# The last expert's down products in an encoder layer with a routed MoE, taken one group of tokens at a time

## The chip, the cores and the metric

One core of one Trainium2 chip. The metric is the device time of one execution in microseconds, the median of several runs.

## What is computed

One encoder layer for two sets of tokens with shared weights, 256 prompt tokens and 512 sample tokens of width 2048: a mixer (latent attention beside a gated DeltaNet), then an expert-choice MoE. Only the MoE's end matters here:

```python
aff = softmax(xt @ w_router)                    # 16 experts
gates, idx = top_k(aff.T, C)                    # C = 2*T/16: 32 prompt and 64 sample tokens for each expert
xe = xt[idx]
h = silu(xe @ w_gate) * (xe @ w_up)             # 2048 -> 1024
ye = (h @ w_down) * gates                       # 1024 -> 2048
out = zeros.at[idx].add(ye)                     # and the residual on top
```

Everything is float32. The 96 tokens of an expert (64 of the sample, 32 of the prompt) are one batch in the kernel, in three groups of 32: groups 0 and 1 are sample tokens, group 2 is the prompt's.

## The kernel before, in words

The program runs five stages one after the other on all engines; the last is `moe` (L2620). It takes the 16 experts in turn.

**Weights.** SP streams them into a ring of six slots (`ring`, RING = 6), 2 MB a unit. The slots lie in two buffers of earlier stages, so the trace names them `wbuf` and `x`. An expert has 12 units: eight of gate and up weights (`load_up`, L2677) and four of down weights (`load_down`, L2686). One unit is two DMAs of 1 MB that count on one semaphore per slot. Before it fills a slot again SP waits (`room`, L2673) until TensorE has used what was there (`s_u`, one count for each unit used) and until the slot's earlier loads have landed. A unit of down weights holds 256 of the 1024 rows of w_down, two steps of 128 rows.

**Order.** The units come in the order: up units of expert e+1, then down units of expert e, in a loop over 15 experts (L2695), and last the four down units of expert 15 (L2698). TensorE follows the same order (L2747 to L2754): up(e+1), down(e), and at the end up(15), down(14), down(15). Its loop body holds two experts, seven rounds of it, so it branches back six times.

**The products.** TensorE is split into four column tiles of 32: a matmul has 32 tokens as its stationary operand and 512 columns of weights as the moving one, and four of them (`j`, J = 4) fill the 128 partitions of one PSUM bank with the four quarters of the 2048 output columns. In the trace each float32 matmul has two records. `down` (L2721) waits for `s_th`, the transposed hidden values `hT`. Then it goes unit by unit: for each unit wait until it has landed (L2725), for each of its two steps and each group g the four matmuls into bank 3 + g (L2733). Each bank sums over eight steps f = 0 to 7. Before a group's first step it waits until DVE has emptied the bank (`s_ye`, L2731).

**After the products.** DVE's `output` (L2796) copies the expert's gates into a column, waits until `ye` is free (`s_free`) and until TensorE has used the fourth down unit (`s_u`, L2801), and scales the three banks into `ye`, one instruction a group (L2803), with a count of `s_ye` after each. POOL's `scatter` (L2836) waits for each group's count on its own and issues one indirect DMA that adds 128 rows of 512 values (32 tokens in four quarters) to `y_sample` or `y_prompt` (L2841). After the third it waits until all three have landed (L2843) and frees `ye`. There is one `ye`, so the scatters of expert 14 must have landed before expert 15's values are scaled.

The first three units of expert 0 were multiplied in part in the stage before; their group 2 is done by the helper `expert_unit` (L719, matmul at L726), whose matmuls into one bank follow one another.

Of the kernel before, what the change touches and what calls it, by code (L numbers as in the profile page):

```python
# [36 lines left out]
NE, FF = 16, 1024  # L37
# [80 lines left out]
class Kernel:  # L118
# [18 lines left out]
    def sb(self, name, shape, dt=F32, ctx=None):  # L137
        return (ctx or self.ctx).enter_context(self.nc.sbuf_tensor(name, shape, dt))

    def sem(self, name, ctx=None):  # L140
        return (ctx or self.ctx).enter_context(self.nc.semaphore(name))


def bcast(ap, axis, n):

    shape = list(ap.unsqueeze(axis).shape)
    shape[axis] = n
    return ap.unsqueeze(axis).to_broadcast(shape)
# [570 lines left out]
def expert_unit(k, u, groups):  # L719

    m = k.ring[u].rearrange("p (x k c j r) -> p x k c j r", x=2, k=2, j=4, r=32)
    for kk in range(2):
        q = 2 * u + kk
        for g in groups:
            for j in range(4):
                last = k.nc.tensor.matmul(k.psum[32 * j:32 * j + 32, g, :].rearrange("p (x c r) -> p x c r", x=2, r=32),  # L726
                                          k.xeT[:, 0, q, 32 * g:32 * g + 32], m[:, :, kk, :, j, :],
                                          start=(q == 0), stop=(q == KD - 1))
    return last
# [1890 lines left out]
def moe(k):  # L2620


    nc, a, ps = k.nc, k.a, k.psum
    UNITS, RING = 12, 6


    G, J = CT // 32, 4

    with ExitStack() as c:
        sb = lambda n, s, dt=F32: k.sb(n, s, dt, c)  # L2630
        sem = lambda n: k.sem(n, c)
        ring = k.ring
        xeT = k.xeT
        h = sb("h", [P, G, FF // J])
        hT = sb("hT", [P, G, FF // P, 32])
# [7 lines left out]
        s_w = k.s_ring  # L2643
        s_u = sem("unit_used")
# [4 lines left out]
        s_th = sem("hidden_transposed")  # L2649
# [3 lines left out]
        s_ye = sem("expert_output")  # L2653
# [12 lines left out]
        loaded = lambda e, w: k.ring_base[w % RING] + e * 64 + 32 * (w // RING + 1)  # L2666

        used = lambda e, w: e * UNITS + w + 1

        with nc.Block() as block:  # L2670
# [29 lines left out]
            @block.tensor  # L2700
            def _(pe):
                def up(ex, e, w0, half, u0=0):
                    for u in range(u0, 8):
                        w = w0 + u
                        if u == 0 and w0:
                            pe.wait_ge(s_xa, ex)
                            pe.wait_ge(s_xd, ex)
                            pe.wait_ge(s_ga, ex + 64)
                            pe.wait_ge(s_h, ex)
                        pe.wait_ge(s_w[w % RING], loaded(e, w))  # L2710
                        m = ring[w % RING].rearrange("p (x k c j r) -> p x k c j r", x=2, k=2, j=4, r=32)
                        for kk in range(2):
                            q = 2 * u + kk
                            for g in range(G):
                                for j in range(J):
                                    last = nc.tensor.matmul(ps[32 * j:32 * j + 32, g, :].rearrange("p (x c r) -> p x c r", x=2, r=32),  # L2716
                                                            xeT[:, half, q, 32 * g:32 * g + 32], m[:, :, kk, :, j, :],
                                                            start=(q == 0), stop=(q == KD - 1))
                        last.then_inc(s_u, 1)

                def down(ex, e, w0):  # L2721
                    pe.wait_ge(s_th, ex + 1)
                    for u in range(4):
                        w = w0 + u
                        pe.wait_ge(s_w[w % RING], loaded(e, w))  # L2725
                        m = ring[w % RING].rearrange("p (k n) -> p k n", k=2)
                        for kk in range(2):
                            f = 2 * u + kk
                            for g in range(G):
                                if f == 0:  # L2730
                                    pe.wait_ge(s_ye, ex * G + g + 1)  # L2731
                                for j in range(J):
                                    last = nc.tensor.matmul(ps[32 * j:32 * j + 32, 3 + g, :], hT[:, g, f, :],  # L2733
                                                            m[:, kk, 512 * j:512 * j + 512], start=(f == 0), stop=(f == 7))
                        last.then_inc(s_u, 1)

                pe.wait_ge(k.s_rest, 3)
                for u in range(HEAD):
                    expert_unit(k, u, (2,)).then_inc(s_u, 1)
                up(0, 0, 0, 0, HEAD)  # L2740
                pe.wait_ge(s_gc, 1)
                for which in range(2):
                    for g in range(G):
                        last = nc.tensor.transpose(ps[:, 3, (which * G + g) * NE:(which * G + g + 1) * NE],  # L2744
                                                   rep[:, which, g].rearrange("e j t -> e (j t)"), k.ident[0:NE, 0:NE])
                last.then_inc(s_tx, 1)
                with pe.Fori(0, NE // 2 - 1) as pair:  # L2747
                    for x in range(2):
                        e = pair * 2 + x
                        up(e + 1, e, 8, 1 - x)  # L2750
                        down(e, e, 16)
                up(NE - 1, NE - 2, 8, 1)
                down(NE - 2, NE - 2, 16)
                down(NE - 1, NE - 1, 8)  # L2754

            @block.scalar
            def _(act):
# [21 lines left out]
            @block.vector  # L2779
            def _(dve):  # L2780
                def pick_tokens(ex, half):
                    pick(k, dve, nc.vector.tensor_copy, k.idx_row, ex, half, PICKED[1].start, PICKED[1].stop).then_inc(s_xd, 1)

                def turn_h(ex):

                    dve.wait_ge(s_h, ex + 1)
                    dve.wait_ge(s_u, ex * UNITS + 8)  # L2787
                    nc.vector.transpose(hT[:].rearrange("p g c t -> p (g c t)"),  # L2788
                                        h[:].rearrange("p g n -> p (g n)")).then_inc(s_th, 1)

                def multiply(ex, ups_used):
                    dve.wait_ge(s_u, ups_used)
                    dve.wait_ge(s_sg, ex + 1)
                    nc.vector.tensor_tensor(h[:], h[:], ps[:, 0:G, 256:512], ALU.mult).then_inc(s_h, 1)  # L2794

                def output(ex, e, w0):  # L2796
                    dve.wait_ge(s_ye, ex * G + G)
                    nc.vector.tensor_copy(gate[:].unsqueeze(2), gates[:, :, bass.ds(ex, 1)]).then_inc(s_gc, 1)  # L2798
                    dve.wait_ge(s_gc, ex + 3)
                    dve.wait_ge(s_free, ex + 1)  # L2800
                    dve.wait_ge(s_u, used(e, w0 + 3))  # L2801
                    for g in range(G):
                        nc.vector.tensor_scalar(ye[:, g, :], ps[:, 3 + g, :], gate[:, g:g + 1], None, ALU.mult).then_inc(s_ye, 1)  # L2803

                for j in range(J):
                    nc.vector.tensor_scalar(rep[:, 0, :, j, :], k.idxf[:].rearrange("e (g t) -> e g t", t=32), float(J), float(j), ALU.mult, ALU.add)
                nc.vector.tensor_copy(rep[:, 1], bcast(k.vals[:].rearrange("e (g t) -> e g t", t=32), 2, J)).then_inc(s_gc, 1)
                dve.wait_ge(s_ga, 64)
                pick_tokens(1, 1)
                dve.wait_ge(s_tx, 1)  # L2810
                nc.vector.tensor_copy(quarter[:].rearrange("p g e -> p (g e)"), ps[:, 3, 0:G * NE])  # L2811
                nc.vector.tensor_copy(gates[:].rearrange("p g e -> p (g e)"), ps[:, 3, G * NE:2 * G * NE]).then_inc(s_gc, 1)  # L2812
                dve.wait_ge(s_gc, 2)
                dve.sem_inc(s_ye, G)
                multiply(0, 8)
                with dve.Fori(0, NE // 2 - 1) as pair:
                    for x in range(2):
                        e = pair * 2 + x
                        pick_tokens(e + 2, x)
                        turn_h(e)  # L2820
                        multiply(e + 1, used(e, 15))
                        output(e, e, 16)
                turn_h(NE - 2)
                multiply(NE - 1, used(NE - 2, 15))
                turn_h(NE - 1)
                output(NE - 2, NE - 2, 16)
                output(NE - 1, NE - 1, 8)

            @block.gpsimd
            def _(pool):  # L2830
# [54 lines left out]
```

## Time and profile before

| | |
|---|---|
| runs | 2944.68, 2947.03, 2947.17 us; median 2947.03 |
| the profiled execution | 2948.12 us, its span 2946.4 us, mean granted TensorE clock 0.981 |
| TensorE matmuls busy | 2781.0 us (94%) |
| VectorE, ScalarE, GpSimd busy | 1102.7 (37%), 603.5 (20%), 604.1 us (21%) |
| MoE stage | from about 1912 us to the end |

Times in the rows are microseconds from the start of the span unless they are marked ns. PE is TensorE, PEld its weight loads, DVE VectorE, ACT ScalarE, POOL GpSimd, SP SyncE; a q behind an engine means its sequencer or DMA queue. L2733 is line 2733 of the kernel. The granted clock is a share of full speed: 1.00 is 2.4 GHz, 0.50 is 1.2 GHz. q1 is the queue of the DMAs that SP issues, q0 that of POOL's indirect DMAs, q8 and q14 fetch instructions. "us to landing" counts from a DMA's issue to the last increment of its semaphore.

### The profile page before, as it was taken

The numbers are of one execution on the slowest core, as the hardware profiler recorded it, in microseconds if no ns is written. First come the engines' busy times: TensorE is split into PE (matmuls) and PEld (weight loads), VectorE is DVE, ScalarE is ACT, GpSimd is POOL, SyncE is SP. The second block draws the span as 40 slices with busy tenths as digits, with TensorE's granted clock in tenths as the row PEclk, the third lists the DMA queues.
The fourth block names the chain that finished last, engine by engine and source line by source line (L and its number), as shares of the span: only waits on it lengthen the run. The fifth ranks groups of instructions, "written<-read, shape, count | busy, mean of one in ns | idle before, by whom it ended". The sixth has DMA issues, their size and how long they took to land. (4 is left out here: it accounts for less than half of the span.)

```text
span 2946.4 us, 53712 instructions
## 1 busy us (share of the span) xinstructions
PE 2781.0 (94%) x18967; PEld 1403.0 (48%) x18967; DVE 1102.7 (37%) x2185; ACT 603.5 (20%) x1790; POOL 604.1 (21%) x969
## 2 busy tenths in 40 slices
PE   8999999999999999989689999999999999999997
PEld 4544455556666676667466445533223232322332
DVE  1145444431674576375676423511111111111110
ACT  4100455412212411320421011211111111111100
POOL 1444111104213221411530000111121121112111
PEclk9999999999999999999799999999999999999999
DMA  7664100021111101200412744799999999999996
GB/s 246 210 229 135 53 24 35 11 95 57 54 49 50 44 21 59 72 16 26 157 44 69 289 171 169 294 424 412 405 403 399 410 404 406 404 404 404 393 409 241
DMA packets 170389, 603.95 MB, mean 205 GB/s; under 512 B 16528, under 2 KB 81896, under 8 KB 116456
## 3 DMA queue, kind: packets, MB, share of 16 engines
q1 hardware_dynamic: 163175, 587.58, 51.5%
q0 software_dynamic: 6912, 12.59, 2.5%
q8 instruction: 161, 2.64, 0.3%
q14 instruction: 141, 1.15, 0.1%
HBM read 554.14 MB, written 45.98 MB: 204 GB/s over the span
## 5 line engine op out<-in xcount | busy, mean ns | idle before, releaser
L2716 PE MATMUL psum<-wbuf 128*32 128x512 f32 x2976 | 335.5, 608 | 25.0 <-issue 23.2
L1444 PE MATMUL psum<-xT,wbuf 128*128 128x512 f32 x720 | 340.2, 611 | 0.3 <-PEq L828 0.3
L2716 PE MATMUL psum<-x,wbuf 128*32 128x512 f32 x3024 | 330.3, 592 | 0.0
L715 POOL COPY wbuf<-xT 128x16 f32 x533 | 114.4, 215 | 780.6 <-issue 415.2
L2716 PEld LDWEIGHTS psum<-wbuf 128*32 128x32 f32 x2976 | 102.7, 112 | 252.5 <-issue 252.5
L715 DVE COPY wbuf<-xT 128x16 f32 x500 | 94.6, 191 | 336.9 <-issue 336.0
L2716 PEld LDWEIGHTS psum<-x,wbuf 128*32 128x32 f32 x3024 | 103.2, 110 | 221.3 <-issue 221.2
L1444 PEld LDWEIGHTS psum<-xT,wbuf 128*128 128x128 f32 x720 | 133.3, 195 | 126.3 <-issue 121.3
L2733 PE MATMUL psum<-x,hT 128*32 128x512 f32 x1584 | 173.0, 592 | 0.0
L715 ACT COPY wbuf<-xT 128x16 f32 x503 | 111.3, 222 | 275.2 <-issue 272.6
L1447 PE MATMUL psum<-xT,wbuf 128*128 128x256 f32 x736 | 165.0, 380 | 0.0
L2733 PE MATMUL psum<-wbuf,hT 128*32 128x512 f32 x1488 | 162.7, 592 | 2.1 <-DVE ye L2803 2.1
L1447 PEld LDWEIGHTS psum<-xT,wbuf 128*128 128x128 f32 x736 | 139.1, 191 | 25.1 <-issue 8.1
L624 PE MATMUL psum<-wbuf,xT 128*128 128x512 f32 (+1 forms) x384 | 141.4, 526 | 0.9 <-DVE xT L453 0.9
L1512 PE MATMUL psum<-inv,mix_g 64*64 64x64 f32 (+1 forms) x2112 | 103.6, 231 | 38.4 <-DVE inv L1911 38.4
L2803 DVE TENSOR_SCALAR ye<-psum,gate 128x512 f32<-128x512 f32 x48 | 33.1, 745 | 280.5 <-PE psum L2733 280.5
L1925 DVE TENSOR_TENSOR inv<-inv,psum 64x256 f32<-64x256 f32 (+1 forms) x264 | 116.7, 442 | 54.9 <-PE psum L1512 51.1
L2765 ACT ACTIVATE h<-psum 128x768 f32<-128x768 f32 x16 | 13.0, 810 | 594.4 <-PE psum L2716 594.4
L1512 PEld LDWEIGHTS psum<-inv,mix_g 64*64 64x64 f32 (+1 forms) x2112 | 88.8, 141 | 94.7 <-DVE inv L1911 76.1
L1916 DVE TENSOR_TENSOR wbuf<-psum,blocks 128x512 f32<-128x512 f32 x144 | 96.6, 688 | 90.8 <-PE psum L1512 87.8
L2276 PE MATMUL psum<-wbuf,xT 128*128 128x512 f32 x260 | 121.2, 606 | 6.3 <-DVE x L2397 5.3
L2276 PE MATMUL psum<-wbuf 128*128 128x512 f32 x288 | 126.1, 595 | 0.0
(327 smaller groups left out, 3599.4 us busy)
## 6 DMA issues: line engine op xcount, KB each, us to landing
x<-in_w_down SPq DMA_DIRECT2D x66, 1024.0 KB, 12.3
wbuf<-in_w_gate SPq DMA_DIRECT2D x65, 1024.0 KB, 9.4
wbuf<-in_w_up SPq DMA_DIRECT2D x65, 1024.0 KB, 16.8
x<-in_w_gate SPq DMA_DIRECT2D x63, 1024.0 KB, 9.7
x<-in_w_up SPq DMA_DIRECT2D x63, 1024.0 KB, 16.5
wbuf<-in_w_down SPq DMA_DIRECT2D x62, 1024.0 KB, 12.3
wbuf<-in_w_in SPq DMA_DIRECT2D x16, 2048.0 KB, 8.9
wbuf<-weight_sums SPq DMA_DIRECT2D x16, 2048.0 KB, 9.0
```

The lines of the kernel that those rows point to most:

```text
L624: last = nc.tensor.matmul(ps[:, u % 3, 0:n], xT[:, d, t * P:(t + 1) * P], wb[g % 2][:, d, 0:n], start=(d == 0), stop=(d == KD - 1))
L715: last = copy(k.xeT[:, half, :, t:t + 1], k.mixT[:, :, cols][:, :, bass.ds(r, 1)])
L1444: last = nc.tensor.matmul(ps[:, b, 0:SS_], wg[:, m % 2, d, h * P:(h + 1) * P], k.xT[:, d, SP_:T], start=(d == 0), stop=(d == KD - 1))
L1447: last = nc.tensor.matmul(ps[:, b + 1, 0:SP_], wg[:, m % 2, d, h * P:(h + 1) * P], k.xT[:, d, 0:SP_], start=(d == 0), stop=(d == KD - 1))
L1512: last = nc.tensor.matmul(ps[lo:hi, x, n * P + lo:n * P + hi], left[lo:hi, x, n, lo:hi], right[lo:hi, x, n, lo:hi], start=True, stop=True)
L1916: nc.vector.tensor_tensor(p1[:, x].rearrange("p (d h) c -> p d h c", d=2), ps[:, x, :].rearrange("p (d h c) -> p d h c", d=2, h=2), bcast( ...
L1925: last = nc.vector.tensor_tensor(o, o, bank[lo:hi, :, lo:hi], ALU.subtract)
L2276: last = nc.tensor.matmul(ps[:, u % 3, :], left, k.slot[v % 3][:, q, :], start=(q == 0), stop=(q == H - 1))
L2716: last = nc.tensor.matmul(ps[32 * j:32 * j + 32, g, :].rearrange("p (x c r) -> p x c r", x=2, r=32), xeT[:, half, q, 32 * g:32 * g + 32], ...
L2733: last = nc.tensor.matmul(ps[32 * j:32 * j + 32, 3 + g, :], hT[:, g, f, :], m[:, kk, 512 * j:512 * j + 512], start=(f == 0), stop=(f == 7))
L2765: nc.scalar.activation(h[:], ps[:, 0:G, 0:256], ACT.Silu).then_inc(s_sg, 1)
L2803: nc.vector.tensor_scalar(ye[:, g, :], ps[:, 3 + g, :], gate[:, g:g + 1], None, ALU.mult).then_inc(s_ye, 1)
```

## The change

TensorE gets a function `last_down` in place of `down` for expert 15. It waits for hT, then for all four units of down weights, and then goes group by group: for each group wait until its bank is empty, all eight steps f, and one count of `s_u` after the group's last matmul. So expert 15's down products count three times on `s_u`, not four. DVE's `output` has a flag for the last expert: with it DVE waits for one more count of `s_u` before each group's scaling, in place of the one wait ahead of all three. POOL and SP are as they were.

```diff
+                def last_down(ex, w0):
+
+                    pe.wait_ge(s_th, ex + 1)
+                    for u in range(4):
+                        pe.wait_ge(s_w[(w0 + u) % RING], loaded(ex, w0 + u))
+                    for g in range(G):
+                        pe.wait_ge(s_ye, ex * G + g + 1)
+                        for f in range(8):
+                            m = ring[(w0 + f // 2) % RING].rearrange("p (k n) -> p k n", k=2)
+                            for j in range(J):
+                                last = nc.tensor.matmul(ps[32 * j:32 * j + 32, 3 + g, :], hT[:, g, f, :],
+                                                        m[:, f % 2, 512 * j:512 * j + 512], start=(f == 0), stop=(f == 7))
+                        last.then_inc(s_u, 1)
+
...
-                down(NE - 1, NE - 1, 8)
+                last_down(NE - 1, 8)
...
-                def output(ex, e, w0):
+                def output(ex, e, w0, last=False):
                     dve.wait_ge(s_ye, ex * G + G)
                     nc.vector.tensor_copy(gate[:].unsqueeze(2), gates[:, :, bass.ds(ex, 1)]).then_inc(s_gc, 1)
                     dve.wait_ge(s_gc, ex + 3)
                     dve.wait_ge(s_free, ex + 1)
-                    dve.wait_ge(s_u, used(e, w0 + 3))
+                    if not last:
+                        dve.wait_ge(s_u, used(e, w0 + 3))
                     for g in range(G):
+                        if last:
+                            dve.wait_ge(s_u, used(e, w0 + g))
                         nc.vector.tensor_scalar(ye[:, g, :], ps[:, 3 + g, :], gate[:, g:g + 1], None, ALU.mult).then_inc(s_ye, 1)
...
-                output(NE - 1, NE - 1, 8)
+                output(NE - 1, NE - 1, 8, True)
```

## Rows read from the trace of the kernel before

**Rows 1.** The page: the chain that ended last, by engine and line

```profile
PE 34%; issue 1%; POOL 0%; DVE 0%; DVEq 0%; POOLq 0%
PE psum L2716 22%; PE psum L2733 11%; PE psum L726 0%; POOL out_y_sample L2841 0%; POOL out_y_prompt L2841 0%; DVE ye L2803 0%; DVE h L2794 0%; DVEq L2670 0%; PE psum L2744 0%; DVE quarter_rows L2811 0%; DVE gate L2798 0%; DVE gates L2812 0%; DVE hT L2788 0%; DVEq L2801 0%; DVEq L2787 0%
```

**Rows 2.** The chain in order of time: start, us, what

```profile
1912.72 5.36 PE psum L726 x48
...
2887.33 20.64 PE psum L2733 x192
...
2909.89 0.14 issue
2910.03 20.84 PE psum L2733 x192
```

**Rows 3.** Timeline of PE, 2885 to 2947: start, us, what, idle before

```profile
2910.03 5.36 PE L2733 MATMUL psum<-wbuf,hT 128*32 128x512 f32 x48 [2.09 <-DVE ye L2803]
```

**Rows 4.** Timelines of DVE and POOL at the end

```profile
2930.99 2.07 DVE L2803 TENSOR_SCALAR ye<-psum,gate 128x512 f32<-128x512 f32 x3 [19.28 <-PE psum L2733]
...
2923.42 0.19 POOL L2837 COPY scatter_rows<-quarter_rows 128x3 uint32<-128x3 uint32 x1 [7.49 <-DMA out_y_prompt<-ye,scatter_rows]
2932.53 1.56 POOL L2841 DMA_INDIRECT out_y_sample<-ye,scatter_rows  x1 [8.93 <-DVE ye L2803]
...
2936.25 1.55 POOL L2841 DMA_INDIRECT out_y_prompt<-ye,scatter_rows  x1 [0.30 <-issue]
```

**Rows 5.** DMA issues, count and us to landing: the first scatter, then the third

```profile
out_y_sample<-ye,scatter_rows POOLq DMA_INDIRECT x1, 4.8
...
out_y_prompt<-ye,scatter_rows POOLq DMA_INDIRECT x1, 5.8
```

**Rows 6.** Loads of w_down for expert 15: units 0 and 3

```profile
L2692 SPq DMA_DIRECT2D wbuf<-in_w_down x2: 338/382/426, 2882.4 to 2882.8; - x2
...
DMA to landing us min/median/max: 12.3/17.1/21.9
...
L2692 SPq DMA_DIRECT2D x<-in_w_down x2: 328/382/435, 2897.8 to 2898.2; - x2
...
DMA to landing us min/median/max: 11.9/17.5/23.1
```

**Rows 7.** Packets by queue: 2913 to 2915, and 2919 to 2921

```profile
q0 software_dynamic: 124, 0.23, 85.3%
q1 hardware_dynamic: 9, 0.06, 6.8%
...
q1 hardware_dynamic: 5, 0.03, 4.1%
```

**Rows 8.** Landing of w_down: the pair at 2867; all 80 loads, 2300 to 2900

```profile
DMA to landing us min/median/max: 12.8/17.5/22.3
...
DMA to landing us min/median/max: 7.2/14.3/23.1
```

**Rows 9.** DMA queues between 2300 and 2900: packets, MB, share of sixteen engines

```profile
q1 hardware_dynamic: 32207, 234.56, 94.6%
q0 software_dynamic: 3888, 7.08, 6.4%
```

**Rows 10.** TensorE's stalls and clock: windows, chain, and waits from 1900 on

```profile
2932.00:2936.00 4.00, 0.00 (x0) 0.00 (x0) 1.06 (x2) 0.00 (x0) 3.11 (x2) 0.65 0.36 33
2075.00:2079.00 4.00, 3.59 (x24) 1.11 (x28) 0.35 (x2) 1.32 (x6) 3.09 (x2) 0.69 1.01 395
...
2075.41 43.10 PE psum L2716 x384
...
2204.72 41.41 PE psum L2716 x384
...
2846.13 41.20 PE psum L2716 x384
...
PE psum L2716 <- issue: 23.2, 6, 4.0
```

In the windows the columns are: length, PE busy (count), PEld, DVE, ACT, POOL, granted clock, share of the DMA engines, GB/s.

## The prediction

> **What bounds the kernel now.** Read the chain that ended last by line first [rows 1]: from the router to the end of the program it is TensorE, on L2716 (gate and up products) and L2733 (down products), 22% and 11% of the span, with 1% of "issue" between. So time is changed by what TensorE waits for, or by what follows its last instruction. The chain in order of time shows that end [rows 2]. Expert 14's down products start at 2887.33. After them TensorE waits 2.09 us [rows 3] for the transposed h and for `ye` to be scaled out of the banks, then runs the last expert's down products from 2910.03 for 20.84 us, 192 records without a pause. Only then come three scalings (2.07 us together), the three scatters, and nothing else. The POOL and DVE timelines [rows 4] show the first scatter issued at 2932.53 and the third at 2936.25, 3.72 us later. The landing view [rows 5] gives 5.8 us from the third issue to landing, so it lands at 2942.05, and the span ends 4.35 us later at 2946.4, with no work in between. The profiled execution took 2948.12 us (1.72 over its span), 1.1 us above the median of 2947.03.
>
> **What the change takes out.** Groups 0 and 1 leave the tail: they are scaled and scattered while TensorE is on the next group. Behind TensorE's last matmul stays one scaling and one scatter. From the start of the first scaling to the first scatter's issue it is now 2932.53 - 2930.99 = 1.54 us [rows 4]; the same 1.54 will stand between TensorE's end and group 2's issue, which today comes 3.72 us later. **Term 1: -3.7 us.** A second gain: today the three scatters queue up on the DMA engines. The first, alone, lands 4.8 us after its issue, the third 5.8 [rows 5]. Seven microseconds apart (20.8 / 3) each is alone. **Term 2: -1.0 us**, between 0 (if the prompt scatter is longer of itself) and -1.0.
>
> **What has no price.** The products are the same: 96 matmuls (192 records), the same weight slices, only reordered. The new order accumulates eight times running into one bank. The trace has that order: the helper at L726 works on group 2 alone, and its 48 records take 5.36 us, as the first 48 of L2733 do [rows 2, 3]. Bounds: -0.2 to +0.2 us on 20.8; I take 0. Weight loads are unchanged in number. One s_u increment of four goes, and nobody waits for a fourth. DVE's wait moves into its loop; nothing is queued behind it, and POOL already waits group by group. `ye` must be free before group 0 is scaled: expert 14's last scatter lands just before 2923.42 [rows 4], and group 0 will be ready no earlier than 2910 + 7 = 2917. At the old start that would hold group 0 some 6 us, still with no effect on group 2 at 2931: hidden. SP's queue is not touched: its last load is issued long before.
>
> **What it adds, and this decides.** A down product for one group sums over all 1024 rows of h, that is over all four weight units. Group by group, therefore, TensorE must have all four before its first matmul is worth starting, and the diff puts all four waits ahead of group 0. Today unit u is needed only at 2910.03 + 5.2 u, so unit 3 at about 2925.6. When do they land? The tile view of w_down gives issue and time to landing of each pair [rows 6]: unit 0 at 2882.8 + 21.9 = 2904.7; unit 3, issued 2897.84 and 2898.2, at 2898.2 + 23.1 = 2921.3. Today that is 4.3 us ahead of its use and costs nothing. With the change TensorE stands until 2921.3, and wakes about 0.1 us after (as 2909.89 to 2910.03 in [rows 2]). **Term 3: 2921.4 - 2910.0 = +11.4 us.**
>
> Is that landing believable, when a pair is 2 MB and its first DMA landed in 11.9 us? The DMA view in small windows [rows 7] says yes: in 2913 to 2915 the weight queue still moves 9 packets, in 2919 to 2921 another 5 (4.1% of sixteen engines, less than the 6.25% of one). A single late engine carries the last pieces, and the scatter of expert 14 (q0, 85.3% of the time in 2913 to 2915) shares it meanwhile. The lateness is no accident of the last pair: the pair issued at 2867 also took 22.3 us, and over 80 loads of w_down the longest is 23.1 [rows 8]. Its cause would be at work without a profile too: between 2300 and 2900 the queues of weights and scatters together fill 94.6 + 6.4 = 101% of the engines [rows 9], so an engine that has fallen behind has no slack to catch up in. Bounds of the landing: 2919.1 (unit 0's 21.9 us in place of 23.1, and 1.0 more because this is one execution) to 2922.5, as much above as the 1.2 between the two. The Trainium skill, page "DMA: Bandwidth & Descriptors", section "Latency and other measured facts", says that two of the sixteen DMA engines are usually slower in traces, as a best guess through the descriptor rings of the software queue. By that rule lateness belongs to the kernel and not to this one execution, and [rows 7] agree that it is one engine.
>
> **Term 4, the clock.** TensorE will stand 13.4 us, from 2887.33 + 20.64 = 2907.97 [rows 2] to 2921.4. After its last matmul today the granted clock is 0.65 over 2932 to 2936 (2.4 GHz at first, then 1.2) [rows 10], so it will be at 1.2 GHz when the products restart. The price of a restart is to be had from the six stalls where TensorE's loop goes round ([rows 10]: 23.2 us together, 3.9 each). After the one before 2075.41 the next 384 records took 43.10 instead of the undisturbed 41.20, with a clock of 0.69 over 2075 to 2079, and so after five of the six; after the one before 2204.72 they took 41.41. So +1.9 us in five, +0.2 in one. A long stand can cost more; I bound it by twice 1.9. I take **+1.9 us**, range +0.2 to +3.8.
> The Trainium skill, page "TensorE: Matmul & The Clock Gate", section "HAM oscillation", advises a loop over all K-tiles of one output tile, so that the engine stays warm. This change is just such a loop, and by that rule term 4 would be 0 and the time 2953.6 us. The rows disagree here, because the K-tiles have not arrived.
>
> **Sum:** -3.7 - 1.0 + 11.4 + 1.9 = **+8.6 us**. Profiled: 2948.1 to 2956.7; against the median, 2947.0 + 8.6 = 2955.6. Ends of this case: least 9.1 + 0.2 - 4.7 = +4.6, most 12.6 + 3.8 - 3.7 = +12.7. A measurement of this kernel can tell about 0.2%, 5.9 us, from no change.
>
> **Rivals.**
> *A, the weights are there sooner in the timed runs.* Mechanism: without a profile the late engine is less late, and the last pair lands as its bulk does. Where: the wait on the fourth unit. For it: one profiled execution stands alone, and the first DMA of the pair landed at 2897.84 + 11.9 = 2909.7. Against it: [rows 8, 9]. Price: at 2913 to 2917 the stand is 3 to 7 us, the restart costs 0.2 to 1.9, and the sum is -1.5 to +4.2, so 2945.5 to 2951: no change that can be told. The point where the change breaks even is a landing of 2914.7 with a warm restart, 2912.8 with a cold one.
> *B, no wait at all,* the change as one would wish it: -4.7 us, 2942.3. It needs all four units by 2910.03, and unit 3's own bulk is at the edge of that. Even this is 0.16%, so faster by over 0.2% asks for noise on top.
> *C, a long cold restart.* If TensorE stayed at 1.2 GHz for all of the last products, term 4 would be up to +20.8 and the time 2974.5. Nothing in the MoE stage does this: after each of the six stalls dense matmuls brought the clock back within one 384-record stretch.
>
> **Chances.** Forecast 0.72, A 0.22, B 0.03, C 0.03. Within the forecast about a tenth (an early landing or a cheap restart) falls below +5.9. Slower 0.67, same 0.30, faster 0.03. The range reaches down from the forecast's least, 2951.6, over most of A to 2947, and up to the forecast's most, 2959.5.
>
> **What the changed profile should show.** In the PE timeline: L2733 ends near 2908, an idle time of some 13 us, and the new line starting near 2921.4 with 192 records in 22 to 23 us; granted clock 0.5 at its start. The end of expert 14's products, the loads of w_down and the scatter of expert 14 unmoved. The first two scatters of the last expert some 7 us apart and inside TensorE's time, the third near 2945.9 with about 4.8 us to landing, and the end of the span near 2955. I am wrong if the new line starts before 2917, if the clock costs over 4 us, or if the third scatter does not come 1.5 us after the last matmul.

## The result, and the profile after

| | before | changed |
|---|---|---|
| runs, median | 2947.17 us (2944.68 to 2952.17, 5 runs) | 2961.66 us (2959.99 to 2964.45, 5 runs) |
| ratio, 95% interval | 1 | 1.0040 (1.0030 to 1.0051): slower, by 0.4% |
| the profiled execution, its span | 2948.12, 2946.4 us | 2960.63, 2958.9 us |
| TensorE busy, mean clock | 2781.0 us (94%), 0.981 | 2784.3 us (94%), 0.978 |

The ratio is +11.8 us on 2947.0 (+8.8 to +15.0). A second set of runs of the changed kernel, told of below, gave 1.0033 (1.0023 to 1.0044), +9.7 us. The forecast was +8.6. The ratios are of fast runs; one execution with the waits alone (11450 us) and one of the changed kernel without scatters (4758 us) are slow runs and in none of them.

The chain of the changed kernel in order of time, from the last load on (start, us, what; L2747 is the new down product of expert 15, L2820 the scaling, L2858 the scatter):

```profile
2900.91 0.33 SPq L2692
2901.24 0.04 issue
2901.28 24.48 DMA x<-in_w_down
2925.76 0.24 issue
2926.01 22.26 PE psum L2747 x192
2948.26 0.03 issue
2948.29 0.76 DVE ye L2820
...
2949.84 1.55 POOL out_y_prompt L2858
```

Here [rows 2] had nothing but TensorE; now one DMA stands in the chain for 24.48 us. It is the second half of the fourth down unit. The waits and the timelines of the changed kernel show the two sides of it:

```profile
PE psum L2747 <- DMA x<-in_w_down: 15.0, 1, 15.0
```

```profile
2900.52 10.49 PE L2733 MATMUL psum<-wbuf,hT 128*32 128x512 f32 x96
2926.01 3.33 PE L2747 MATMUL psum<-wbuf,hT 128*32 128x512 f32 x16 [15.00 <-DMA x<-in_w_down]
...
2936.20 1.56 POOL L2858 DMA_INDIRECT out_y_sample<-ye,scatter_rows  x1 [8.64 <-DVE ye L2820]
2942.97 1.55 POOL L2858 DMA_INDIRECT out_y_sample<-ye,scatter_rows  x1 [5.21 <-DVE ye L2820]
2949.84 1.55 POOL L2858 DMA_INDIRECT out_y_prompt<-ye,scatter_rows  x1 [5.32 <-DVE ye L2820]
```

TensorE stands 15.00 us where [rows 3] had 2.09. Behind it the tail is what the change was made for: the first two scatters lie inside TensorE's time, and the third comes 1.6 us after the last matmul. Against [rows 4], where the third came 5.4 us after, that is 3.8 us. It lands in 4.7 us instead of 5.8 [rows 5].

The granted clock of the changed kernel in the same stretch (windows: length, PE busy, PEld, DVE, ACT, POOL, granted clock, share of the DMA engines, GB/s):

```profile
2916.00:2920.00 4.00, 0.00 (x0) 0.00 (x0) 0.00 (x0) 0.00 (x0) 2.70 (x2) 0.50 0.94 140
...
2924.00:2926.00 2.00, 0.00 (x0) 0.03 (x1) 0.00 (x0) 0.00 (x0) 0.00 (x0) 0.50 0.06 15
2926.00:2928.00 2.00, 2.00 (x12) 0.65 (x16) 0.00 (x0) 0.00 (x0) 0.19 (x1) 0.50 0.03 5
2928.00:2930.00 2.00, 2.00 (x16) 0.49 (x12) 0.00 (x0) 0.00 (x0) 0.00 (x0) 0.77 0.00 0
2930.00:2932.00 2.00, 2.00 (x24) 0.67 (x20) 0.00 (x0) 0.00 (x0) 0.00 (x0) 1.00 0.00 0
```

At 2924 to 2926 one engine's worth of DMA (0.06) is all that moves: TensorE waits for the late engine alone. When it starts, the clock is at 1.2 GHz, and full again at 2930.

The difference of the two profiled spans is 12.5 us, of which 3.0 is no part of the change. Expert 14's products end at 2911.0 here (the row of their last 96 records above: start 2900.52, 10.49 us) and at 2908.0 before, with the same work up to there; 4.4 us of difference stood already at the first MoE products of the chain (1917.10, and 1912.72 in [rows 2]). Executions of one program differ by that much. So from here on times are also counted from the end of expert 14's products to the end of the span, 38.4 us before and 47.9 changed: +9.5 us.

### The profile page after: what moved, and what is told of

Its sections match the earlier page's. It is cut to its first block and busy times, and to the rows that moved or that the text cites. A ratio compares the mean times of both kernels' runs of the same rounds, so it can differ in the third digit from the quotient of the medians.

```text
span 2958.9 us, 53714 instructions
## 1 busy us (share of the span) xinstructions
PE 2784.3 (94%) x18967; PEld 1397.1 (47%) x18967; DVE 1100.9 (37%) x2185; ACT 603.4 (20%) x1790; POOL 601.5 (20%) x969
## 5 line engine op out<-in xcount | busy, mean ns | idle before, releaser
L2716 PEld LDWEIGHTS psum<-x,wbuf 128*32 128x32 f32 x3024 | 101.7, 110 | 222.8 <-issue 222.6
L2733 PE MATMUL psum<-x,hT 128*32 128x512 f32 x1440 | 157.3, 592 | 0.0
L2820 DVE TENSOR_SCALAR ye<-psum,gate 128x512 f32<-128x512 f32 x48 | 33.3, 745 | 293.2 <-PE psum L2733 261.2
## 6 DMA issues: line engine op xcount, KB each, us to landing
x<-in_w_gate SPq DMA_DIRECT2D x63, 1024.0 KB, 10.3
```

## The experiments

Theory W: what the change adds is the stand (TensorE idle until the fourth unit has landed) and a cold restart (its first matmuls behind the stand at 1.2 GHz); what it gives is 4.8 us in the tail. The rival, O: the new order is slow in itself, or the gain in the tail isn't there. A second question came with W: why is one DMA engine late? S: through the scatters of the software queue. E: of itself.

### The waits alone, in the old order

```diff
+                for u in range(4):
+                    pe.wait_ge(s_w[(8 + u) % RING], loaded(NE - 1, 8 + u))
                 down(NE - 1, NE - 1, 8)
```

> The kernel before with one edit: TensorE waits for all four down units of expert 15 ahead of its down products, which keep their old order. Theory W (what the change adds is the stand until the fourth unit has landed, and a cold restart): TensorE stands about 15 us after expert 14's products instead of 2.1, its 192 records take about 22.3 us instead of 20.8, the three scatters stay 1.86 us apart behind them, and the time is that of the kernel before +12.9 + 1.4 = +14.3 us, some 4.8 us above the changed kernel. Theory O (the new order itself is slow, accumulating eight times in one bank, or the later part of the program moved by chance): no stand of more than 3 us and the time of the kernel before within 2 us.

Measured: ratio 1.0054 (1.0041 to 1.0067), +15.9 us (+12 to +20). Its chain in order of time:

```profile
2894.79 21.59 DMA x<-in_w_down
2916.38 0.31 issue
2916.69 22.25 PE psum L2733 x192
```

And its row in the timeline of PE:

```profile
2916.69 6.75 PE L2733 MATMUL psum<-wbuf,hT 128*32 128x512 f32 x48 [12.17 <-DMA x<-in_w_down]
```

The stand is 12.17 us in this execution, the records take 22.25 in the old order too, and from the end of expert 14's products to the end it is 49.8 us, +11.4, where the landing came 2.9 us sooner after that end than in the changed kernel (11.9 against 14.8). In the profiles the wait without the new order costs more than the two together; the intervals of the timed ratios overlap. O falls: the old order with the waits loses as the new one does.

### The waits where group 0 first uses each unit

```diff
-                    for u in range(4):
-                        pe.wait_ge(s_w[(w0 + u) % RING], loaded(ex, w0 + u))
                     for g in range(G):
...
                         for f in range(8):
+                            if g == 0 and f % 2 == 0:
+                                pe.wait_ge(s_w[(w0 + f // 2) % RING], loaded(ex, w0 + f // 2))
```

> The changed kernel, but TensorE waits for each down unit where group 0 first uses it. Theory W: group 0 starts about 2 us after expert 14's products as before, stands once before its seventh step until the fourth unit lands (about 6 to 7 us), and the last matmul comes 15.5 us after that landing instead of 22.3: about +7.5 us against the kernel before at TensorE's end, less 4.8 in the tail, +2.7, and up to 1.4 more if the clock falls. Theory O: no better than the changed kernel, +12.

Measured: 1.0016 (1.0007 to 1.0026), +4.7 us (+2 to +8). TensorE stood 1.94 us for the third unit and 5.73 for the fourth, and 144 records behind it took 18.51 us, with the restart cold (at full clock 144 take 15.66, as in the next experiment):

```profile
2912.60 1.92 PE L2747 MATMUL psum<-wbuf,hT 128*32 128x512 f32 x16 [2.05 <-DVE hT L2802]
2914.32 1.93 PE L2747 MATMUL psum<-x,hT 128*32 128x512 f32 x16
2918.18 1.92 PE L2747 MATMUL psum<-x,hT 128*32 128x512 f32 x16 [1.94 <-DMA x<-in_w_down]
2925.84 3.64 PE L2747 MATMUL psum<-x,hT 128*32 128x512 f32 x16 [5.73 <-DMA x<-in_w_down]
```

The third unit's wait was left out of the expectation. About half of the loss is gone with the place of the waits alone (+4.7 us of +11.8 or +9.7 by the runs; +5.9 of +9.5 or +11.2 by the profiles, from the end of expert 14's products to the end), and the rest stays, since three quarters of group 0 are all that can go ahead of the fourth unit.

### Only the fourth unit group by group

```diff
+                    for u in range(3):
+                        pe.wait_ge(s_w[(w0 + u) % RING], loaded(ex, w0 + u))
+                        m = ring[(w0 + u) % RING].rearrange("p (k n) -> p k n", k=2)
+                        for f in (2 * u, 2 * u + 1):
+                            for g in range(G):
+                                if f == 0:
+                                    pe.wait_ge(s_ye, ex * G + g + 1)
+                                for j in range(J):
+                                    nc.tensor.matmul(ps[32 * j:32 * j + 32, 3 + g, :], hT[:, g, f, :],
+                                                     m[:, f % 2, 512 * j:512 * j + 512], start=(f == 0), stop=False)
-                    for u in range(4):
+                    for u in range(3, 4):
                         pe.wait_ge(s_w[(w0 + u) % RING], loaded(ex, w0 + u))
                     for g in range(G):
-                        pe.wait_ge(s_ye, ex * G + g + 1)
-                        for f in range(8):
+                        for f in range(6, 8):
```

> Expert 15's units 0 to 2 in the old order over all groups, and only the fourth unit (steps 6 and 7) group by group. Theory W: no stand, since that unit has landed 4 us before it is used; groups end 1.7 us apart, less than the 1.86 between scatters, so the third scatter is issued 1.6 to 1.9 us after the last matmul instead of 5.4 and lands in about 5.8 as before: -3.5 to -3.8 us, faster than the kernel before by 0.12%. Theory O: the tail's gain is not there, the time of the kernel before or more.

> The kernel with only the fourth unit group by group, once more on another set of rounds: -3.6 us against the kernel before, 0.9988, where the first set gave 0.9994 (0.9985 to 1.0003).

Measured: both sets 0.9994 (0.9985 to 1.0003), -1.8 us with an interval that takes in no change: the gain of some 3.6 us that was expected is not shown by the runs. The profile of the first set shows the mechanism whole. The end of its chain:

```profile
2927.52 1.75 PE psum L2756 x16
2929.27 0.03 issue
2929.30 0.05 DVEq L2828
2929.34 0.05 issue
2929.39 0.76 DVE ye L2829
...
2930.93 0.88 POOL out_y_sample L2867
...
2932.80 0.73 POOL out_y_sample L2867
...
2934.65 1.55 POOL out_y_prompt L2867
```

No DMA stands in it, though the fourth unit landed late here as well, at 2924.7: it was used at 2927.5. Scalings of the groups lie inside TensorE's time, and the chain leaves TensorE after the first group's records. From the end of expert 14's products (2909.8) to the end of the span (2944.7) it is 34.9 us, 3.5 less than before. The profile of the second set has the same chain at the end, and 36.3 us there, only 2.1 less than before: behind a wait of 2.10 us, as long as the one in [rows 3], the clock fell (0.50 over 2912 to 2914), and the first 48 records took 7.05 us instead of 5.36.

```profile
2910.46 7.05 PE L2748 MATMUL psum<-wbuf,hT 128*32 128x512 f32 x48 [2.10 <-DVE ye L2829]
```

By its profiles this is the best kernel of the study that computes everything; its runs can't tell it from the kernel before.

### Two units group by group

The same with 2 in place of 3: units 0 and 1 in the old order, units 2 and 3 by groups, both waited for first.

> Units 0 and 1 in the old order, units 2 and 3 group by group with both waits ahead of group 0. Theory W: TensorE gets there 10.3 us after its start, 1.0 to 2.4 us before the fourth unit lands, and stands that long, the clock staying at full; groups end 3.4 us apart, the scatters hardly meet, and the third lands in 4.8 to 5.8: -4.8 to -3.8 in the tail, +1.0 to +2.4 for the stand, about -2.5 us against the kernel before. Theory O: the time of the kernel before or more.

Measured: 0.9994 (0.9986 to 1.0003). The stand is there, and at 2.78 us somewhat longer than the 1.0 to 2.4 expected:

```profile
2927.24 11.86 PE L2756 MATMUL psum<-x,hT 128*32 128x512 f32 x96 [2.78 <-DMA x<-in_w_down]
```

96 records took 11.86 us where 10.3 is usual, so the clock fell (0.50 over 2927 to 2929), which was not expected. From the end of expert 14's products (2911.9) to the end (2949.8) it is 37.9 us, 0.5 less than before, where 2.5 had been expected; the runs can't tell either from no change.

### TensorE kept busy while it would stand

28 groups of four matmuls of unit 0 into a bank that nobody reads, ahead of the four waits.

```diff
+                    pe.wait_ge(s_w[w0 % RING], loaded(ex, w0))
+                    m = ring[w0 % RING].rearrange("p (k n) -> p k n", k=2)
+                    for n in range(28):
+                        for j in range(J):
+                            nc.tensor.matmul(ps[32 * j:32 * j + 32, 6, :], hT[:, 0, n % 2, :],
+                                             m[:, n % 2, 512 * j:512 * j + 512], start=True, stop=True)
```

> The changed kernel, with 28 groups of four matmuls (12.0 us at full clock) of unit 0 into a bank that nobody reads, put ahead of the wait for the four units, so that TensorE is busy while it would stand. Theory W: the down products start when the fourth unit has landed, no earlier and no later than in the changed kernel (at most 1 us later where the landing comes early), and at full clock: 20.8 us instead of 22.3, so 1.0 to 1.5 us less than the changed kernel. If the clock is not what made them 22.3, they stay so.

Measured: 1.0064 (1.0047 to 1.0081). The filler was sized wrongly: 0.43 us is the time of four records, and four matmuls are eight. It ran 24.24 us and held the products until 2935.7, ten after the landing. Read is only that the products then took 20.64 us. So once more with 14 groups:

> The same with 14 groups of matmuls ahead of the wait, since one group turned out to take 0.86 us and not 0.43: TensorE is busy for 12.0 of the 15 us. The down products start when the fourth unit has landed, as in the changed kernel, and take 20.8 us or less instead of 22.3: 1.4 us below the changed kernel. If they take 22 again, the clock term is not the cold restart.

Measured: 1.0025 (1.0016 to 1.0035).

```profile
2914.03 12.22 PE psum L2744 x112
2926.25 20.64 PE psum L2753 x192
```

The unit landed at 2924.8, so the filler overran it by 1.4 us and gave back what the clock gained in this execution. The time bears it out only loosely: beside the second set of the changed kernel (1.0033) it is 2.4 us less, with intervals that overlap. But the term is clean in the profiles: 20.64 us at full clock, against 22.26 in the changed kernel, 23.40 in its second profiled execution, 22.25 with the waits alone and 23.56 without expert 14's scatters (below). Cold restart: +1.6 to +2.9 us.

### Without the scatters of the other experts

Two pairs of kernels, changed and before, each without the indirect DMAs of experts 0 to 14; the output lacks those experts.

```diff
                     for g in range(G):
                         wait_apart(pool, s_ye, ex * G + G + g + 1, k)
+                        if not (isinstance(ex, int) and ex == NE - 1):
+                            continue
                         nc.gpsimd.indirect_dma_start(...)
-                    pool.wait_ge(s_sc, ex * 16 * G + 16 * G)
+                    if isinstance(ex, int) and ex == NE - 1:
+                        pool.wait_ge(s_sc, 16 * G)
```

> The changed kernel without the indirect DMAs of experts 0 to 14; their part of the output is left out. It asks what makes one DMA engine late. Theory S (the software queue's scatters slow that engine): the last pair of w_down lands with its bulk, 5 us or less after the end of expert 14's products instead of 12 to 15, and the stand shrinks to 2 to 5 us; time 8 to 12 us below the changed kernel. Theory E (the engine is slower of itself or through the fetching of instructions): it lands 9 us or more after that end, and the time is within 4 us of the changed kernel.

> The kernel before without the indirect DMAs of experts 0 to 14; their part of the output is left out. Beside the changed kernel without them it shows what the change gives when no unit is late. Theory: it has the tail of the kernel before (third scatter 5.3 us after the last matmul, 10 us to the end), so it is 4.8 us above the changed kernel without scatters (2944.2), at about 2949, and 1 to 2 us below the kernel before.

Measured: changed kernel without scatters 0.9977 (0.9967 to 0.9987) of the kernel before, -6.8 us; the kernel before without scatters 0.9997 (0.9988 to 1.0006). Its loads of w_down over 2300 to 2900, then the last pair of the changed kernel without scatters, in the view of w_down:

```profile
DMA to landing us min/median/max: 5.4/7.6/9.9
...
L2692 SPq DMA_DIRECT2D x<-in_w_down x2: 328/381/434, 2902.4 to 2902.8; - x2
...
DMA to landing us min/median/max: 7.5/8.9/10.3
```

The longest landing is 9.9 us where [rows 8] had 23.1. The last pair lands at 2902.8 + 10.3 = 2913.1, half a microsecond after the end of expert 14's products (2912.6), not 12 to 15 after. TensorE waits for nothing new:

```profile
2914.62 1.92 PE L2747 MATMUL psum<-wbuf,hT 128*32 128x512 f32 x16 [2.10 <-DVE ye L2820]
```

So S holds against E: the engine is late because of the scatters. The lateness also grows from expert to expert. The same view of w_down's landings over 1900 to 2060, 2400 to 2570 and 2740 to 2900, in the kernel before and then in the changed kernel without scatters:

```profile
DMA to landing us min/median/max: 9.1/11.2/13.9
DMA to landing us min/median/max: 7.6/14.0/19.1
DMA to landing us min/median/max: 7.8/15.7/23.1
...
DMA to landing us min/median/max: 8.1/11.3/13.7
DMA to landing us min/median/max: 6.2/8.1/9.9
DMA to landing us min/median/max: 5.5/7.5/9.5
```

What these runs do not part is whether it is the scatters' load or something in their own queue: without them all queues together hold 97.6% of the engines over 2300 to 2900, with them 101.7%.

The gain over the changed kernel is larger than the 8 to 12 us expected: by the profiles 17.9 us from the end of expert 14's products to the end (47.9 to 30.0). The stand gives 12.9 of it, the warm restart 1.4, and 3.7 come from the end of the program, which was not foreseen (last section). The kernel before without scatters has these 3.7 us as well, so it is the one to compare with. Between those two the change does what its tail promises: 30.0 us from the end of expert 14's products to the end of the span against 34.8, -4.8 us, and 0.9977 to 0.9997 by the runs, -5.9, with intervals that just fail to meet.

### Without expert 14's scatters only

The same for expert 14 alone; the output lacks that expert.

> The changed kernel without the three indirect DMAs of expert 14 alone; its part of the output is left out. Theory: the last twelve packets or so of the late engine share it with these scatters (one in 0.48 us instead of 0.31), so without them the landing comes 1.5 to 2.5 us earlier, and the rest of the lateness, built up before, stays: about 10 to 12 us from the end of expert 14's products, time 1.5 to 2.5 us below the changed kernel. If the lateness were made by these scatters alone, it would land within 5 us of that end.

Measured: 1.0023 (1.0013 to 1.0033), beside 1.0040 and 1.0033 of the changed kernel. The unit landed 12.5 us after the end of expert 14's products: 2899.79 + 22.22 = 2922.01, against 2909.5.

```profile
2899.79 22.22 DMA x<-in_w_down
2922.01 0.24 issue
2922.25 23.56 PE psum L2747 x192
```

The lateness is thus built up before, over the experts ahead. What these three scatters add can be read from the weight queue's last packets. The DMA views of the changed kernel over 2918.5 to 2925.5, then of this one over 2915.5 to 2921.8:

```profile
q0 software_dynamic: 265, 0.48, 48.4%
q1 hardware_dynamic: 16, 0.11, 4.1%
...
q1 hardware_dynamic: 23, 0.16, 6.2%
```

With the scatters 16 packets take 7.0 us, without them 23 take 6.3, and one engine of sixteen (6.25%) then does nothing else. From this I estimate 16 x (0.44 - 0.27) = 2.7 us for these scatters. The landing itself can't confirm it: it came 11.9 to 15.2 us after that end in the executions that have them, and 12.5 lies among those. By the runs it is 3 to 5 us less than the changed kernel, with intervals that overlap.

### The changed kernel again

> The changed kernel again, beside the others on one chip: +9 to +12 us against the kernel before.

Measured: 1.0033 (1.0023 to 1.0044). Stand 15.48 us, records 23.40, landing 15.2 us after the end of expert 14's products, and 49.6 us from there to the end of the span, +11.2.

```profile
2896.12 24.96 DMA x<-in_w_down
2921.08 0.24 issue
2921.32 23.40 PE psum L2747 x192
```

## Why the prediction was right

The forecast was slower, by the wait for the fourth unit, 2955.6 us against 2947.0 (ratio 1.0029). The ratio measured was 1.0040 and 1.0033; by the median of 2961.66 alone the time lies 2.2 us above the upper end of the range, by the ratio on the median that was shown (2958.8) inside. Term by term, in profiled executions, counted from the end of expert 14's products:

| term | forecast | measured |
|---|---|---|
| 1, two groups leave the tail | -3.7 | -3.8 (third scatter 1.6 us after the last matmul, 5.4 before) |
| 2, the third scatter alone on the DMA engines | -1.0 | -1.1 (4.7 us to landing, 5.8 before) |
| 3, the stand | +11.4 | +12.9 (15.0 instead of 2.1; the landing 14.8 us after that end, not 13.4, and 0.24 to wake, not 0.1), +13.4 in the second profiled execution |
| 4, the cold restart | +1.9 | +1.4 (22.26 instead of 20.84), +2.6 in the second |
| sum | +8.6 | +9.4, and +11.1 |

- *The price of the new order is nothing.* Right: without scatters the records take 20.84 us in either order of groups, and behind a stand 22.25 in the old order and 22.26 in the new.
- *The wait decides.* Right, shown by putting it alone into the old order (+15.9 us), and by taking its cause away (without scatters the new order is 5.9 us faster than the old one by the runs, 4.8 by the profiles).
- *Term 3 was sized from a single execution,* 13.4 us from the end of expert 14's products to the landing. Ten profiled executions with all scatters in place, the one of before among them, had 11.9, 11.9, 13.4 and seven of 14.7 to 15.2. The execution before was on the early side, and that is most of why the loss came out 1 to 3 us larger than forecast. My bounds, 11 to 14.5, were too narrow above. And the longest of the 80 landings in [rows 8] is that of this very pair, so it was no second witness (without it the longest is 22.3); the longest landings grow over the stage, from 13.9 to 23.1, and the last pair is the worst placed.
- *That the lateness holds in the timed runs (rival A against the forecast).* Right: the timed difference is as large as the profiled one. The reason I gave was only half the cause. I argued from full DMA queues, 101% with the scatters, which leave a late engine no slack. Without scatters the weight queue alone still holds 96.9% over the same stretch, and the lateness is gone. So the scatters are needed for it; that the slack of 2 to 3% which comes back without them plays no part is not shown. The Trainium skill's "DMA: Bandwidth & Descriptors", section "Latency and other measured facts", names the software queue as its best guess for slower engines. The runs without scatters agree with it, but don't show its mechanism, and which engine it is no run here shows.
- *The clock's rule.* The products restarted at a granted clock of 0.50. The Trainium skill's "TensorE: Matmul & The Clock Gate", section "HAM oscillation", advises a loop over all K-tiles of one output tile so that the engine stays warm; that loop did not keep it warm here. The same section says that a wait for a DMA lets the clock fall and the next products start cold, and this agrees with every stand of 12 us or more here. (By the advice as the prediction applied it the time comes to 2947.0 + 6.7 = 2953.7, not 2953.6.)
- *Rival C, cold throughout.* Not seen: in the changed kernel the clock was full again at 2930, four microseconds after the start.

## What to carry to other kernels

Before a loop is turned so that one output is finished early, ask what a finished output needs: here the sum runs over all of the streamed units, so turning the loop moves the use of the last unit from three quarters of the way in to the first quarter, and the wait ahead of it to the start. Read the time to landing of that very transfer to its last piece, not the rate of the queue. Turn only the part of the loop that follows the last arrival: the fourth unit by groups waits for nothing, and gave 3.5 and 2.1 of the 4.8 us in two profiled executions, which is too little for these runs to tell from no change.

## What the runs showed of the hardware that was not expected

- With scatters that hold 6.4% of the DMA engines' time [rows 9], the landings of w_down come later from expert to expert, and at the end one engine of sixteen is left with the last pieces; without them the longest landing of w_down over 2300 to 2900 falls from 23.1 to 9.9 us, and the median from 14.3 to 7.6.
- The end of the program: with 48 scatters the span ends 4.4 us after the last landing (2949.84 + 4.7 to 2958.9 in the changed kernel), with three scatters 0.7 us (2937.04 + 4.9 to 2942.6). Nothing is shown in that time, and its cause stays open.
- A stand of 2.78 us was followed by a stretch at the lower clock (96 records in 11.86 us), and so was one of 2.10 (48 records in 7.05 instead of 5.36), while one of 3.81 in the kernel before cost 0.2 us [rows 10] and one of 2.09 nothing in its first 48 records [rows 3]. The dearest was one of 3.78 in the changed kernel: 384 records behind it took 43.90 us instead of 41.20. The cost of a short stand varies from none to 2.7 us, and no run here tells why.
